# The layers' output projection as seven block products per pair of weight pieces

## The reference, cut to what matters

```
for l in range(2):
    ...
    y_rg = rglru(...) * silu(rg_z)                 # 256 x 1024
    y_ml = mlstm_branch(...) * silu(ml_z)          # 256 x 1024
    y = concatenate([y_rg, y_ml], axis=-1) @ w_out[l]   # (256 x 2048) @ (2048 x 1024)
    x = x + gate[:, None, :] * y
return rms_norm_2(x, final_g)
```

## Time and profile before

| | us |
|---|---|
| median of the runs | 1009.26 |
| the profiled execution | 1002.76 |
| its span | 1000.9 |
| PE busy | 920.2 (92%) |
| DVE busy | 402.6 (40%) |
| L1006, 512 records of PE | 111.2 |
| granted TensorE clock, mean | 0.962 |

### The profile page before, as it was taken

One profiled execution on the slowest core, in us unless ns is written; L12 is line 12 of the kernel. 1 busy time (PEld: TensorE's weight loads), 2 busy tenths in 40 slices (PEclk: granted clock), 3 DMA queues, 4 the chain that ended last, 5 costly groups with the idle time before them and its releaser, 6 DMA issues.

```text
span 1000.9 us, 13533 instructions
## 1 busy us (share of the span) xinstructions
PE 920.2 (92%) x5294; PEld 731.2 (73%) x5294; DVE 402.6 (40%) x912; ACT 261.4 (26%) x587; POOL 66.1 (7%) x87
## 2 busy tenths in 40 slices
PE   8889998799799977777799999999999999999997
PEld 7658876688666544443488888788888888878886
DVE  4473656475522111111452462644225246263422
ACT  2244422201212111110318143122011814312201
POOL 5523100002000000000200000000000000000011
PEclk9889999999799989897899999999999999999999
DMA  9845965399699999999454444233433534422311
GB/s 347 324 169 223 381 234 234 126 376 422 258 419 422 420 420 421 420 421 420 163 130 186 138 157 165 88 119 113 148 127 127 189 129 166 157 96 86 131 58 43
DMA packets 35124, 229.52 MB, mean 229 GB/s; under 512 B 5984, under 2 KB 6016, under 8 KB 8176
## 3 DMA queue, kind: packets, MB, share of 16 engines
q1 hardware_dynamic: 30944, 222.05, 57.2%
q0 software_dynamic: 1312, 4.71, 1.4%
q10 hardware_dynamic: 2800, 1.85, 0.6%
HBM read 227.54 MB, written 1.06 MB: 228 GB/s over the span
## 4 chain that ended last, share of the span: by engine, by line
PE 79%; SPq 8%; DMA 4%; DVE 4%; issue 2%; ACT 2%; DVEq 0%; ACTq 0%; POOL 0%; POOLq 0%
PE bank L419 27%; PE bank L1006 11%; SPq L1031 8%; PE bank L869 6%; PE bank L847 6%; PE bank L718 4%; PE bank L625 3%; PE bank L889 3%; DMA s<-in_w_up 3%; PE bank L694 2%; PE bank L754 2%; PE bank L733 2%; PE bank L457 2%; PE bank L904 1%; PE bank L970 1%
## 5 line engine op out<-in xcount | busy, mean ns | idle before, releaser
L419 PE MATMUL bank<-hT,ring 128*128 128x256 f32 x1152 | 260.9, 386 | 0.2 <-ACT s L1150 0.2
L419 PEld LDWEIGHTS bank<-hT,ring 128*128 128x128 f32 x1152 | 220.7, 193 | 35.9 <-issue 3.5
L1006 PE MATMUL bank<-ring,s 128*128 128x256 f32 x512 | 111.2, 379 | 0.0
L1006 PEld LDWEIGHTS bank<-ring,s 128*128 128x128 f32 x512 | 97.1, 190 | 13.1
L1701 DVE SCALAR_TENSOR_TENSOR z<-z,bank 128x256 f32<-128x256 f32 x9 | 3.8, 421 | 156.3 <-ACT z L1246 156.2
L718 PE MATMUL bank<-s,z 128*32 128x256 f32 (+1 forms) x544 | 52.1, 433 | 12.4 <-DMA s<-in_w_up 4.5
L869 PE MATMUL bank<-ring,hT 128*128 128x256 f32 x256 | 56.4, 380 | 0.0
L847 PE MATMUL bank<-hT,ring 128*128 128x256 f32 x256 | 55.6, 379 | 0.0
L869 PEld LDWEIGHTS bank<-ring,hT 128*128 128x128 f32 x256 | 48.3, 190 | 7.3 <-issue 0.9
L847 PEld LDWEIGHTS bank<-hT,ring 128*128 128x128 f32 x256 | 48.5, 190 | 6.5
L718 PEld LDWEIGHTS bank<-s,z 128*32 128x32 f32 (+1 forms) x544 | 29.3, 127 | 28.8 <-issue 20.7
(11 more groups left out here) (393 smaller groups left out, 1347.8 us busy)
## 6 DMA issues: line engine op xcount, KB each, us to landing
ring<-in_layer_pieces SPq DMA_DIRECT2D x64, 1024.0 KB, 4.8
ring<-in_first_pieces SPq DMA_DIRECT2D x49, 1024.0 KB, 7.8
s<-in_w_gate SPq DMA_DIRECT2D x17, 1024.0 KB, 16.6
s<-in_w_up SPq DMA_DIRECT2D x17, 1024.0 KB, 14.2
s<-in_w_down SPq DMA_DIRECT2D x11, 1024.0 KB, 26.5
ring<-in_w_down SPq DMA_DIRECT2D x11, 1024.0 KB, 18.8
ring<-in_w_gate SPq DMA_DIRECT2D x10, 1024.0 KB, 21.2
ring<-in_w_up SPq DMA_DIRECT2D x9, 1024.0 KB, 19.4
```

The source lines that it names most:

```text
L419: mm = pe.matmul(b[:, 0:T], w[:, (k0 + kb) * CW + m * P:(k0 + kb) * CW + (m + 1) * P], rhs[:, kb, :], start=(kb == 0), stop=(kb == nk - 1))
L1006: mm = pe.matmul(xo[j, tt][:, 0:CW], yT[:, kb, tt * P:(tt + 1) * P], w[:, kb, :], start=(kh == 0 and kb == 0), stop=(kh == 1 and kb == KB ...
```

## The change

Per layer, half `p` of the output columns (two pieces wide) and half `kh` of the contraction there is a block product of 2 by 2 blocks: rows of tile 1 and tile 0, the two halves of four 128-blocks of the contraction, and the two pieces. Eight block products (four matmuls each) gave its four results. The change computes them by seven block products, from four sums of row blocks (`S1` to `S4`) and four of weight blocks (`T1` to `T4`), which DVE makes in SBUF. `T1` overwrites its piece, the others go to buffers that are free by then. The seven products of `kh` 0 and 1 add up in seven banks. ACT copies the first product out of PSUM; DVE forms the four results from the seven banks with seven additions and takes them on as before. In layer 0 and 1 alike the first pair (`p` 0, `kh` 0) runs six products, and its second product runs later, after the first of (0, 1). The transposes of `hh` go through two banks with four transposes each in place of four banks with two. PE waits, at the start, for all its banks of pool `A`. In `OUT_ORDER` the two pieces of a pair become neighbours. `gfin2` moves to another buffer.

```diff
+OUT_ORDER = ((0, 0), (0, 1), (1, 0), (1, 1), (0, 2), (0, 3), (1, 2), (1, 3))
+PRODUCTS = (("A11", "B11"), ("A12", "B21"), ("S2", "T2"), ("S3", "T3"), ("S1", "T1"), ("A22", "T4"), ("S4", "B22"))
+Y_BANKS = (7, 4)
+X_ORDER = ((1, 0), (0, 1), (0, 0), (1, 1), (1, 2), (0, 3), (0, 2), (1, 3))
+def of_weights(wa, wb, extra):
+    t3, t2, t4 = extra
+    return {"B11": wa[:, 0:4, :], "B21": wa[:, 4:8, :], "B12": wb[:, 0:4, :], "T1": wb[:, 0:4, :], "B22": wb[:, 4:8, :],
+            "T3": t3, "T2": t2, "T4": t4}
+def of_rows(yT, sums):
+    return {"A11": yT[:, 0:4, P:T], "A12": yT[:, 4:8, P:T], "A21": yT[:, 0:4, 0:P], "A22": yT[:, 4:8, 0:P],
+            "S1": sums[:, 0], "S2": sums[:, 1], "S3": sums[:, 2], "S4": sums[:, 3]}
...
@@ PE @@
+                pe.wait_ge(A.free, A.put)
+                def product(p, kh, i, ys, ws):
+                    r, w = PRODUCTS[i]
+                    for kb in range(4):
+                        if (p, kh) == (0, 1) and i < 2:
+                            pe.wait_ge(Y.free, Y.upto(f"ym{l}{(4 * i + kb) // 2}"))
+                        mm = pe.matmul(product_at(p, i), ys[r][:, kb, :], ws[w][:, kb, :],
+                                       start=(kh == 0 and kb == 0), stop=(kh == 1 and kb == 3))
+                    return mm
+                for p in range(2):
+                    for kh in range(2):
+                        if (p, kh) == (0, 1):
+                            pe.wait_ge(S["hq_ready"], l + 1)
+                            pe.wait_ge(B.free, B.put)
+                            for n in range(KB // 2):
+                                b = Y.acquire(pe, f"ym{l}{n}")
+                                ...
+                        for i in range(7):
+                            if (p, kh, i) == (0, 0, 1):
+                                continue
+                            if (p, kh, i) == (0, 1, 1):
+                                pe.wait_ge(Y.free, Y.upto(f"ym{l}2"))
+                                product(0, 0, 1, *late_product).then_inc(chunk_used, 1)
+                            if i in (2, 5):
+                                pe.wait_ge(S["sums_ready"], 4 * pair + (3 if i == 2 else 4))
+                            if i in (2, 3, 6):
+                                pe.wait_ge(S["row_sums_ready"], 8 * l + 4 * kh + (2 if i == 2 else 3 if i == 3 else 4))
+                            if (p, kh) == (1, 0) and i == 1:
+                                pe.wait_ge(S["first_copied"], 2 * l + 1)
+                            if (p, kh) == (1, 0) and i in (2, 3):
+                                pe.wait_ge(S["x_part"], 8 * l + (1 if i == 2 else 4))
+                            mm = product(p, kh, i, ys, ws)
...
@@ ACT @@
+            def first_copy(l, p):
+                act.wait_ge(S["product_done"], 14 * l + 7 * p + 1)
+                step(f(parts[0], product_at(p, 0), ACT.Copy), S["first_copied"])
...
@@ DVE @@
+                def weight_sums(p, kh):
+                    ...
+                    step(tten(w["T3"], w["B22"], w["B12"], ALU.subtract), S["sums_ready"])
+                    step(tten(w["T1"], w["B12"], w["B11"], ALU.subtract), S["sums_ready"])
+                    step(tten(w["T2"], w["B22"], w["T1"], ALU.subtract), S["sums_ready"])
+                    step(tten(w["T4"], w["B21"], w["T2"], ALU.subtract), S["sums_ready"])
+                def row_sums(kh):
+                    y = of_rows((thr, ymT)[kh], row_sums_of[kh])
+                    step(tten(y["S1"], y["A21"], y["A22"], ALU.add), S["row_sums_ready"])
+                    ...
@@ DVE, in the loop over heads, after the z_jobs @@
+                    if h == 0:
+                        weight_sums(0, 0)
+                    if h == 1:
+                        row_sums(0)
@@ DVE, after the scaling of hh @@
+                weight_sums(0, 1)
                 for m in range(KB):
-                    b = B.take(v)
-                    step(stt(ymT[:, m, :], b[:, 0:T], colM[:, l, 8 + m:9 + m], zm[:, m, :], ALU.mult, ALU.mult), B.free)
+                    i = m % 2
+                    if i == 0:
+                        b = Y.take(v)
+                    step(stt(ymT[:, m, :], b[:, i * T:(i + 1) * T], colM[:, l, 8 + m:9 + m], zm[:, m, :], ALU.mult, ALU.mult),
+                         Y.free if i else None)
+                row_sums(1)
+                weight_sums(1, 0)
                 if l + 1 < LAYERS:
                     modulation(l + 1)
...
+                def combine(p):
+                    p1, top, low, last, c11 = parts
+                    ...
+                    v.wait_ge(S["first_copied"], 2 * l + p + 1)
+                    step(tten(c11, product(1), p1, ALU.add))
+                    add_to_x(4 * p, c11)
+                    step(tten(top, product(2), p1, ALU.add))
+                    step(tten(low, product(3), top, ALU.add))
+                    step(tten(top, product(4), top, ALU.add))
+                    step(tten(last, product(4), low, ALU.add))
+                    add_to_x(4 * p + 1, last)
+                    step(tten(low, product(5), low, ALU.add))
+                    add_to_x(4 * p + 2, low)
+                    step(tten(top, product(6), top, ALU.add))
+                    add_to_x(4 * p + 3, top)
+                combine(0)
+                weight_sums(1, 1)
+                combine(1)
```

More of the change, by code:

```diff
@@ L305, in build @@
         rows = s2[0:MLH, 0:8 * T].rearrange("p (r t) -> p r t", r=8)
-        gfin2 = s0[:, 0:D]
+        gfin2 = s5[:, 0:D]
+        quarter = lambda s: s.rearrange("p (k c) -> p k c", k=4)
+        extra_of = [[quarter(s) for s in (z0[:, 0:1024], z0[:, 1024:2048], s5[:, 1024:2048])],
+                    [quarter(s) for s in (s0[:, 0:1024], s0[:, 1024:2048], w4[:, :])]]
+        row_sums_of = [s[:, 0:2048].rearrange("p (i k t) -> p i k t", i=4, k=4) for s in (s2, s7)]
+        parts = [tmp[:, 256 + CW * i:256 + CW * (i + 1)] for i in range(5)]
         xf = s3[:, 0:2048].rearrange("p (t d) -> p t d", t=TT)
         stats, moments, ms1 = rt[:, 80:104], rt[:, 104:108], rt[:, 108:110]
-        gated = tmp[:, 256:768].rearrange("p (t c) -> p t c", t=TT)
         zth = (tmp[:, 0:T], tmp[:, 1546:1546 + T])
@@ L333, in build @@
         C = Banks(psum[4:6], sem("c_done"), sem("c_free"))
+        Y = Banks([psum[i] for i in Y_BANKS], sem("y_done"), sem("y_free"))
         slot_full = [sem(f"slot_full{i}") for i in range(RING + 12)]
@@ L988, in _ @@
                 assert not z_left
[L989 to L1007, removed]
-                        if kh == 1:
[L1009 to L1013, removed]
@@ new lines, in _ @@
+                pe.wait_ge(A.free, A.put)
+                assert B.bank(B.put) is psum[Y_BANKS[1]] and B.bank(B.put - 1) is psum[Y_BANKS[0]]
+                def product(p, kh, i, ys, ws):
[6 more added lines that the diff above has]
+                    return mm
@@ L1279, in _ @@
             roots(small[:, 2:4])
+            def first_copy(l, p):
+                act.wait_ge(S["product_done"], 14 * l + 7 * p + 1)
+                step(f(parts[0], product_at(p, 0), ACT.Copy), S["first_copied"])
             def layer_squares(l):
[L1283 to L1289, removed]
+                for n, (tt, j) in enumerate(X_ORDER):
+                    if n % 4 == 0:
+                        first_copy(l, n // 4)
+                    act.wait_ge(S["x_part"], l * 8 + n + 1)
+                    step(f(squares[:, tt, j * CW:(j + 1) * CW], x[:, tt, j * CW:(j + 1) * CW], ACT.Square,
+                           accum_out=part_sq[:, 4 * tt + j:4 * tt + j + 1]), S["ssq_ready"])
+                    if n >= 6:
+                        roots(small[:, 2 + tt:3 + tt])
             for l in range(LAYERS):
@@ L1884, in _ @@
                 z_job()
+                def weight_sums(p, kh):
+                    na, nb = (chunk_of["out2", l, kh, 2 * p + i] for i in range(2))
+                    for n in (na, nb):
+                        v.wait_ge(slot_full[slot[n]], fill_value[n])
+                    if p == 1:
+                        v.wait_ge(*chunk_free[chunk_of["out2", l, kh, 1]])
+                    w = of_weights(full(slots_of[slot[na]]), full(slots_of[slot[nb]]), extra_of[kh])
+                    step(tten(w["T3"], w["B22"], w["B12"], ALU.subtract), S["sums_ready"])
[5 more added lines that the diff above has]
+                    step(tten(y["S1"], y["A21"], y["A22"], ALU.add), S["row_sums_ready"])
+                    step(tten(y["S2"], y["S1"], y["A11"], ALU.subtract), S["row_sums_ready"])
+                    step(tten(y["S3"], y["A11"], y["A21"], ALU.subtract), S["row_sums_ready"])
+                    step(tten(y["S4"], y["A12"], y["S2"], ALU.subtract), S["row_sums_ready"])
                 def weigh(h):
@@ L1923, in _, with add_to_x @@
                 v.wait_ge(S["gate_loaded"], 16 * (l + 1))
[L1924 to L1941, removed]
+                def add_to_x(n, c):
+                    tt, j = X_ORDER[n]
+                    cs = slice(j * CW, (j + 1) * CW)
```

(19 more changed lines are left out.)

35 lines of the change are left out of this document (31 added, 4 removed).

## The result

The changed kernel took 1016.7 us, the median of four runs (1016.23 to 1019.94), against 1008.93 us before; the ratio of the runs is 1.0092, with a 95% interval of 1.0069 to 1.0115. The change makes the kernel slower, by 7.8 us between the medians. The forecast was 7.5 us and 1016.8 us.

The account below looks back on a forecast made before the run. PE, busy 92% of the span, was taken as the bound. Of 13.8 us removed, 13.1 go into waiting: -0.7 + 3.4 (clock) + 4.8 (layer ends) = +7.5 us, 1016.8 us on the median 1009.26; range 1009.5 to 1021.5.

Parts of the forecast that it names:

- three terms: Over both layers: stall against removed products -0.7 us, half clock +3.4 us, later end of each layer +4.8 us.
- The slack of `hq_ready`: Projection: normed `hh` had 1.8 us slack; after six products PE waits from 694.4 to 695.9 us, 1.6 with the release.
- The stall behind `weight_sums(0, 1)`: Transposes of `hh`: DVE's sums delay their emptying, PE idles 4.5 us; net with removed products about -0.35 us per layer.
- The clock: After the 4.5 us stall PE runs at 1.2 GHz for some 3.4 us, losing 1.7 us per layer.
- The end of each layer: DVE is in tile 0's norm when the last product is ready: 2.17 us later in layer 0, 2.63 in layer 1.
- E + 1.81: Layer 0's end: time DVE can take the last product, E being that product's end; before, DVE started at E + 0.1.
- What was called hidden: `weight_sums(0, 0)`, `row_sums`, later weight sums, `combine(0)` and loads delay nothing; margin 0.4 us for the first, 2 us for `combine(0)`.
- The first (the clock holds): Rival: the clock does not fall after the stall; 4.1 us are left, 1013.4 us; chance 0.13.
- the second (sums at one-source speed): Rival: DVE's weight sums take 0.753 us each, PE idles 2.6 us, the clock holds; +0.3 us, 1009.6 us; chance 0.08.
- The third: Rival: the clock falls at the end of layer 0 too, 1.7 us more, 1018.5 us; chance 0.17.
- the unseen: No place named: something not foreseen happens; chance 0.07.

Follow-up runs that it names:

- early sums: Changed kernel, with DVE making the weight sums of (0, 1) before its wait for the squares, not after `hq_ready`: 1002.71 us, ratio 0.9940.
- filled wait: Changed kernel, with 10 additional matmuls (results unused) in PE's second wait, between the second and third group of transposes: 1011.29 us, ratio 1.0009.
- split norm: Changed kernel, with DVE requesting tile 0's root between the last product's addition and gating, and ending both norms after the last addition to `x`: 1012.45 us, ratio 1.0039.
- early squares: Changed kernel plus split norm; ACT squares each head's tiles at once, DVE makes only T3 and T1 before emptying the transposes: 1000.82 us, ratio 0.9922.

## Why the prediction was right

The mechanism was as forecast, and so were the places and the order of size of its three terms. That the total agrees to 0.1 us is luck: layer 0 came out 0.24 us under its forecast and layer 1 0.23 us over it, and within each layer the stall was 0.3 to 0.5 us dearer and the stretch behind it 0.5 us cheaper than forecast.

- **The slack of `hq_ready`.** Forecast: PE is through with six products 1.6 us too early. Measured 1.53 us, and 1.73 in layer 1.
- **The stall behind `weight_sums(0, 1)`.** Forecast 4.5 us of idle time, measured 4.98. The sums took 1.23 us each, as interpolated. The difference is in the transposes: I took a group at 0.72 us from 16 in 2.87 us, but that time held DVE's handing back of banks. Free of it, eight took 1.09 us, so PE was idle sooner. The early sums show that this one place in the order costs 7.3 us of wait and 3.1 us of clock.
- **The clock.** Forecast 1.7 us per layer, from waits of the same length elsewhere. Shown by filling the wait: 1.5 us per layer. The stretch was longer than forecast, 4.3 us of work and not 3.4, so half of it would be 2.1 us. Of this, 1.2 us were lost in the products. In the transposes only 0.4 us were lost of a possible 1.0, because at full clock PE waits 0.38 us for DVE between the last two groups (the filled wait shows it). The length is not fixed: after the same kind of wait the half clock lasted 3.0, 3.5, 4.3 and 5.6 us of PE's time in different traces.
- **The end of each layer.** Forecast +2.17 and +2.63, measured +2.16 and +2.89. DVE took the last product of layer 0 at E + 1.80 us, as forecast (E + 1.81). In layer 1 nearly all of the excess is one gating (L2025, at 1004.34) of 0.66 us instead of 0.42, last section. That it is DVE's order and not only the added addition is shown by the split norm, for 2.0 of the 5.05 us. The other 3 us are argued from the timeline, not taken away by a run.
- **What was called hidden.** `weight_sums(0, 0)`, `row_sums`, the other weight sums and the loads: PE shows no wait in (1, 0) or (1, 1), and DVE none for a piece. DVE's `weight_sums(0, 0)` and the weighing behind it left 0.5 us of its idle time, where 0.4 was forecast. With DVE's work moved later, in the kernel with the early squares, the cover of `combine(0)` was gone.
- **The rivals.** The first (the clock holds) is refuted by the trace, the second (sums at one-source speed) by 1.23 us. The third, the fall of the clock at the end of layer 0, did not happen in the changed kernel: there the clock read 1.00 after 1.82 and 1.26 us. It did happen in three of the experiments, after one wait of 2.4 us.
- **A slip in the chances.** They are split with 0.12 for the first rival and 0.08 for the unseen, where 0.13 and 0.07 were given. It changes no conclusion.

Why executions differ by up to 8.7 us in the part before the change stays open; no experiment here touched it. The traces show where some of it arises: DMA waits of other lengths, and stretches of half clock in other places. The kernel before and the changed one are 2.3 us apart at 73 us and 5.0 us apart at 180 us.

## What to carry to other kernels

Work taken from the bound engine pays only if the next thing that engine waits for is ready earlier as well: here six products ran out 1.5 us before the normed rows came, and the helper's new work stood on the chain to what followed. Put such helper work where the helper waits itself, here the same four instructions before the wait for the squares instead of behind it, worth 10.4 us. And count a long wait of TensorE twice, once for its length and once for the clock after it; if it can't be removed, matmuls without use in it were worth 3.1 us (two waits of 4.98 us) and 1.6 us (one of 2.4 us). The price of the clock differs between executions, so read it from more than one stretch.

## What the runs showed of the hardware that was not expected

A wait of 2.4 us sufficed for the clock to fall in three kernels and not in a fourth; 2.14 us in the kernel with the early sums did not. The kernel before had one fall after 1.65 us and none after 1.19, nor after one of 2.45 us at 192.38. In the changed kernel a wait of 2.81 us that ended at 44.89 left it at 1.00. The length of the wait alone doesn't decide.

The clock also fell where PE had no wait at all. PE's timeline in layer 1, in the kernel before and, behind the dots, in the one with the early sums:

```profile
901.57 1.96 PE L959 MATMUL bank<-s,onesr 4*128 4x512 f32 x4
903.46 4.55 PE L970 MATMUL bank<-s 128*128 128x256 f32 x16
...
906.63 1.96 PE L985 MATMUL bank<-s,onesr 4*128 4x512 f32 x4
908.52 2.88 PE L996 MATMUL bank<-s 128*128 128x256 f32 x16
```

In the kernel before PE was busy without a break from 873.19 us on, and yet the granted clock read 0.50 from 904.2 to 907.6 us; the same 16 records took 4.55 us instead of 2.88. In both kernels the work just ahead was four transposes of 4x4 and two products over only four rows (L959, L985). The half clock followed it in four of ten traces, and in six it did not; in layer 0 of the kernel before the same 16 records took 2.88 us. What decides stays open.

Beside POOL's multiplication of the same time (L2174), DVE's gating of 256 elements in SBUF took 0.66 instead of 0.42 us, three times in layer 1 of the changed kernel, while the instruction that reads a PSUM bank beside it kept its time:

```profile
1003.87 0.43 DVE L2054 TENSOR_TENSOR tmp<-bank,tmp 128x256 f32<-128x256 f32 x1
...
1003.98 0.73 POOL L2174 TENSOR_TENSOR s<-x,s 128x256 f32<-128x256 f32 x1 [4.88 <-DVE x L2026]
...
1004.34 0.66 DVE L2025 TENSOR_TENSOR tmp<-tmp,gateB 128x256 f32<-128x256 f32 x1
```

It goes both ways. The multiplication at 983.04, which began 0.1 us behind a sum of 1024 elements on DVE, took 1.70 us instead of 0.73, and the sum after that one 1.64 us instead of 1.23.
